# Two-layer FFN, GLA and retention block with an attention block: the sums of seven-product pairs divided anew between VectorE, GpSimd and adding DMAs

## The chip, the core and the metric

The kernel runs on one core of one Trainium2 chip. The metric is the device time of one execution in microseconds (us), as the median of repeated runs. Everything is float32 at the interfaces; nothing is shared with other cores.

## What is computed

The input is one sequence of 256 tokens of width 1024. The first block has two layers; each is FFN, mixer, FFN, with a layer norm after each. The mixer is gated linear attention (GLA) in the first layer and retention in the second. A second block follows: three attention branches, their merge, and a further FFN. The change touches the four FFNs of the first block alone:

```python
def swiglu(x, w_in, w_out):
    gate, up = jnp.split(x @ w_in, 2, axis=-1)
    return (jax.nn.silu(gate) * up) @ w_out

def first_block(x, ffn_w_in, ffn_w_out, ln_g, ln_b,
...
    for i in range(DEPTH):
        h = layer_norm(DN_ALPHA * h + 0.5 * swiglu(h, ffn_w_in[i, 0], ffn_w_out[i, 0]), ln_g[i, 0], ln_b[i, 0])
...
        h = layer_norm(DN_ALPHA * h + 0.5 * swiglu(h, ffn_w_in[i, 1], ffn_w_out[i, 1]), ln_g[i, 2], ln_b[i, 2])
```

The width of an FFN's hidden layer is 2816.

## The kernel before

**Tiles and parts.** All weights come as a stream of tiles of 128 x 2048 float32 (1 MB), read by DMAs of the SyncE queue into raw slots. Each float32 is computed with as two reduced parts: ScalarE writes the hi part of a tile (`split_hi`, line 609), VectorE writes lo = raw - hi (`split_lo`, line 1174), and TensorE adds three products, hi by hi, hi by lo and lo by hi. The activations are split in the same way. A tile can be multiplied by its hi part as soon as ScalarE is done, and by its lo part as soon as VectorE is.

**An FFN** has 11 steps of 256 hidden columns (f = 0 to 3 counts the FFNs). A step computes gate and up, `hidden` (line 1293) multiplies silu(gate) by up on VectorE, TensorE transposes the result (`turn_hidden`, line 2209), ScalarE and VectorE split it again (`hidden_hi`, `hidden_lo`), and a `down` product (lines 1988 to 1992) adds it into the output. Steps 0, 1, 4, 7 and 10 are computed in one of the plain ways. In `features_both` (lines 2097 and 2101) the hi weights are multiplied by x hi and x lo side by side, 512 columns, and the lo weights by x hi, 256 columns; ScalarE then copies the half that belongs to x lo out of PSUM and VectorE adds it to the other half (`summed_step`, line 1350), before the silu. In `features_unit` three products of 256 columns add up in PSUM, with no copy and no sum.

**Pairs.** Steps 2 and 3, 5 and 6, 8 and 9 (`GROUPS`) are computed as pairs, each as a product of two 2 x 2 block matrices with seven block products instead of eight. For this, sums of weight tiles and sums of blocks of x are needed. With b11, b12, b21 and b22 the four weight tiles of a pair, the operands of the products are, in order,

- product 1: b11; product 2: t1 = b11 + b12; product 3: b21; product 4: t2 = t1 + b22; product 5: b22; product 6: t3 = t2 - b11; then a down product; product 7: t4 = t2 + b21 in b21's place; then the second down product.

Each sum is made in the raw slot of one of its operands, and is then split into hi and lo as any other tile. The other operands of products 2, 4, 5 and 6 are the four "forms", combinations of blocks of x, with a hi and a lo part each, which all three pairs of an FFN share. `product` (lines 2236, 2237 and 2240) issues eight matmuls with the hi tile, then waits for lo and issues four.

**Who makes the sums before.** t1: an adding DMA in GpSimd's queue (`add_t1`, lines 500 to 506), issued when both tiles have landed. t2 and t3: VectorE (lines 1344 and 1368). t4: an adding DMA in GpSimd's queue (`add_t4`, lines 508 to 513). The form sums and form lo's: VectorE (lines 1322 to 1327, and 1334); the form hi's: ScalarE (line 689).

**What sets the order.** Each engine works through its own queue in the order in which the program is written, and waits on semaphores. Around the first pair, ScalarE's order in an FFN is: the hi of step 1's second tile, the four blocks of x kept in SBUF (`keep_x`, line 672; not in the first FFN), b11's hi, the silu of step 0, the four form hi's, t1's hi, step 0's hidden hi, step 1's copies and silu, b21's hi. GpSimd's queue also has the layer norms' inverse roots, the residuals (line 485), a part of one lo split (line 475), and the DMAs that load the next norm's rows (line 480).

## Time and profile before

| | |
|---|---|
| median of 3 runs | 1524.89 us (1524.52 to 1525.26) |
| the profiled execution: own time, and span of its instructions | 1523.43 us, 1521.5 us |
| TensorE matmuls (PE) | 1490.0 us, 98% of the span |
| VectorE (DVE) | 1112.7 us, 73% |
| ScalarE (ACT) | 833.1 us, 55% |
| GpSimd (POOL) | 156.4 us, 10% |
| mean granted TensorE clock | 0.994 |
| chain of waits that ended last | PE 83%, DVE 7%, DMA 6% |
| adding DMAs from a raw_more slot, to landing | 20 of 1 MB, median 7.2 us |
| adding DMAs from a raw slot, to landing | 4 of 1 MB, median 12.3 us |

The profile follows one execution. In a line of a timeline stand the start, the duration, the engine, the line of the kernel, the operation, output<-inputs with shapes, and in brackets the idle time of the engine before it and what ended that; xN stands for N such instructions in a row. Only the time in which the engine with the most work stands still, here TensorE, is time that could be saved without taking work off it. The granted clock is a share of 2.4 GHz; at 0.50 TensorE runs at 1.2 GHz.

### The profile page before, as it was taken

The numbers are of one execution on the slowest core, as the hardware profiler recorded it, in microseconds if no ns is written. First come the engines' busy times: TensorE is split into PE (matmuls) and PEld (weight loads), VectorE is DVE, ScalarE is ACT, GpSimd is POOL, SyncE is SP. The second block draws the span as 40 slices with busy tenths as digits, with TensorE's granted clock in tenths as the row PEclk, the third lists the DMA queues.
The fourth block names the chain that finished last, engine by engine and source line by source line (L and its number), as shares of the span: only waits on it lengthen the run. The fifth ranks groups of instructions, "written<-read, shape, count | busy, mean of one in ns | idle before, by whom it ended". The sixth has DMA issues, their size and how long they took to land.

```text
span 1521.5 us, 18598 instructions
## 1 busy us (share of the span) xinstructions
PE 1490.0 (98%) x7654; PEld 1258.1 (83%) x7654; DVE 1112.7 (73%) x1135; ACT 833.1 (55%) x839; POOL 156.4 (10%) x152
## 2 busy tenths in 40 slices
PE   8899999989999999999999989999999999999997
PEld 6688888878888788888888868888898888888886
DVE  5887687787877977787567787867686556785555
ACT  5656467565565665554434556555636566354443
POOL 0400020110002000024021200002002200020000
PEclk9999999999999999999999999999999999999999
DMA  9777454477837777555544677746444434465551
GB/s 356 268 231 229 182 204 169 150 262 277 295 106 296 218 241 256 166 227 188 179 160 169 224 249 226 269 163 237 154 167 142 164 139 166 166 222 194 193 191 58
DMA packets 46595, 310.08 MB, mean 204 GB/s; under 512 B 5568, under 2 KB 6016, under 8 KB 10800
## 3 DMA queue, kind: packets, MB, share of 16 engines
q1 hardware_dynamic: 38592, 270.35, 47.8%
q0 software_dynamic: 6112, 34.80, 9.9%
q10 hardware_dynamic: 1808, 3.74, 0.6%
q8 instruction: 61, 1.00, 0.3%
q14 instruction: 22, 0.18, 0.0%
HBM read 282.60 MB, written 1.05 MB: 186 GB/s over the span
## 4 chain that ended last, share of the span: by engine, by line
PE 83%; DVE 7%; DMA 6%; issue 1%; ACT 1%; POOL 1%; SPq 0%; POOLq 0%; DVEq 0%; ACTq 0%
PE psum L1988 16%; PE psum L1992 15%; PE psum L1991 15%; PE psum L2097 7%; PE psum L2124 6%; PE psum L2101 4%; DVE weights_lo L1174 4%; DMA weights_raw_more<-weights_raw_more 3%; PE psum L2240 3%; PE psum L2237 3%; PE psum L2236 3%; PE psum L2131 3%; DMA weights_raw_more<-in_weights 2%; PE psum L2020 1%; PE psum L2033 1%
## 5 line engine op out<-in xcount | busy, mean ns | idle before, releaser
L1174 DVE TENSOR_TENSOR weights_lo<-weights_raw,weights_hi 128x2048 fp32r<-128x2048 f32 x191 | 440.9, 2312 | 198.0 <-ACT weights_hi L609 196.6
L609 ACT ACTIVATE weights_hi<-weights_raw 128x2048 fp32r<-128x2048 f32 (+1 forms) x198 | 372.4, 1883 | 194.9 <-PE psum L1992 136.2
L1174 DVE TENSOR_TENSOR weights_lo<-weights_raw_more,weights_hi 128x2048 fp32r<-128x2048 f32 x56 | 128.2, 2289 | 70.5 <-ACT weights_hi L609 70.5
L1988 PE MATMUL psum<-weights_hi,hidden_hi 128*128 128x512 f32 x416 | 163.9, 394 | 3.3 <-DVE weights_lo L1174 3.3
L1991 PE MATMUL psum<-weights_lo,hidden_hi 128*128 128x512 f32 x416 | 162.4, 390 | 0.0
L1992 PE MATMUL psum<-weights_hi,hidden_lo 128*128 128x512 f32 x416 | 162.1, 390 | 0.0
L1988 PE MATMUL psum<-weights_hi,operand 128*128 128x512 f32 x384 | 151.5, 394 | 0.0
L1991 PE MATMUL psum<-weights_lo,operand 128*128 128x512 f32 x384 | 149.8, 390 | 0.0
L609 ACT ACTIVATE weights_hi<-weights_raw_more 128x2048 fp32r<-128x2048 f32 x56 | 107.1, 1913 | 70.1 <-DMA weights_raw_more<-weights_raw_more 39.2
L1992 PE MATMUL psum<-weights_hi,operand 128*128 128x512 f32 x352 | 137.2, 390 | 0.0
L2097 PE MATMUL psum<-operand,weights_hi 128*128 128x512 f32 x544 | 129.4, 390 | 0.0
L2097 PEld LDWEIGHTS psum<-operand,weights_hi 128*128 128x128 f32 x544 | 101.2, 188 | 20.4
L2124 PE MATMUL psum<-operand,weights_hi 128*128 128x512 f32 x384 | 96.5, 393 | 0.0
L1988 PEld LDWEIGHTS psum<-weights_hi,hidden_hi 128*128 128x128 f32 x416 | 78.2, 188 | 20.4 <-issue 5.2
L1992 PEld LDWEIGHTS psum<-weights_hi,hidden_lo 128*128 128x128 f32 x416 | 78.1, 188 | 16.3
L1991 PEld LDWEIGHTS psum<-weights_lo,hidden_hi 128*128 128x128 f32 x416 | 78.2, 188 | 15.2
L1988 PEld LDWEIGHTS psum<-weights_hi,operand 128*128 128x128 f32 x384 | 72.1, 188 | 15.8 <-issue 1.3
L1991 PEld LDWEIGHTS psum<-weights_lo,operand 128*128 128x128 f32 x384 | 72.2, 188 | 14.2
L2124 PEld LDWEIGHTS psum<-operand,weights_hi 128*128 128x128 f32 x384 | 69.4, 189 | 13.3 <-issue 0.3
L1992 PEld LDWEIGHTS psum<-weights_hi,operand 128*128 128x128 f32 x352 | 66.1, 188 | 13.9
L1174 DVE TENSOR_TENSOR weights_lo_more<-weights_raw_more,weights_hi_more 128x2048 fp32r<-128x2048 f32 x32 | 73.4, 2292 | 1.7 <-ACT weights_hi_more L609 1.7
L2101 PEld LDWEIGHTS psum<-operand,weights_lo 128*128 128x128 f32 x544 | 69.7, 191 | 2.6
(386 smaller groups left out, 2799.9 us busy)
## 6 DMA issues: line engine op xcount, KB each, us to landing
weights_raw<-in_weights SPq DMA_DIRECT2D x198, 1024.0 KB, 4.8
weights_raw_more<-in_weights SPq DMA_DIRECT2D x56, 1024.0 KB, 8.9
weights_raw_more<-weights_raw_more POOLq DMA_DIRECT2D x20, 1024.0 KB, 7.2
ln_rows<-in_ln_rows POOLq DMA_DIRECT2D x16, 512.0 KB, 7.3
weights_raw_more<-weights_raw POOLq DMA_DIRECT2D x4, 1024.0 KB, 12.3
weights_raw<-in_weights SPq DMA_DIRECT2D x4, 256.0 KB, 4.3
weights_raw<-in_weights SPq DMA_DIRECT2D x2, 512.0 KB, 6.7
normalised<-in_x POOLq DMA_DIRECT2D x2, 512.0 KB, 11.1
```

The costliest lines, as they stand in the source:

```text
L609: nc.scalar.activation(hi[:, rest], whole[:, rest], ACT.Copy).then_inc(hi_split, 1)
L1174: nc.vector.tensor_tensor(lo_of(n), raw_of(n), hi_of(n).bitcast(F32), ALU.subtract).then_inc(lo_split, 1)
L1988: mm(out, a_hi, b_hi, start=start, stop=False, skip_group_check=True)
L1991: mm(out, a_hi, b_lo, start=False, stop=False, skip_group_check=True)
L1992: return mm(out, a_lo, b_hi, start=False, stop=stop, skip_group_check=True)
L2097: mm(banks[b // 2][:, b % 2, :], w_hi_n[:, cols], x_both[:, c, :, :].rearrange("p a t -> p (a t)"), start=c == 0, stop=False, skip_group_c ...
L2101: last = mm(banks[b // 2][:, b % 2, 0:TOK], w_lo_n[:, cols], x_hi[:, c, :], start=False, stop=c == KC - 1, skip_group_check=True)
L2124: mm(banks[half][:, b, :], w_hi_n[:, cols], x_both[:, c, :, :].rearrange("p a t -> p (a t)"), start=c == 0, stop=False, skip_group_check=True)
L2131: last = mm(banks[half][:, b, 0:TOK], w_lo_n[:, cols], x_hi[:, c, :], start=False, stop=c == KC - 1, skip_group_check=True)
L2236: mm(work[:, b, :], a_hi, w_hi_n[:, cols], start=start and k == 0, stop=False, skip_group_check=True)
L2237: mm(work[:, b, :], a_lo, w_hi_n[:, cols], start=False, stop=False, skip_group_check=True)
L2240: last = mm(work[:, b, :], a_hi, w_lo_n[:, cols], start=False, stop=k == 3, skip_group_check=True)
```

## The change

The form sums (now five instructions) and the four form lo's go from VectorE to GpSimd (`first_forms`), in all four FFNs. t1 goes from an adding DMA to VectorE (`add_t1`), t3 from VectorE to GpSimd (`add_t3`); t2 stays on VectorE, t4 an adding DMA. Step 1 goes from `features_both` to `features_unit`. ScalarE makes the form hi's in the order 0, 3, 2, 1. Line numbers of the changed kernel are 2 to 26 higher.

```diff
+FORM_ORDER, FORM_SUMS = (0, 3, 2, 1), (1, 5, 4, 2)
...
                     for tb in range(TB):
                         residual(tb, ALPHA if ln < 6 else ALPHA_2)
-                    if LAYER_STARTS[ln] in FFN_STARTS:
-                        add_t1(LAYER_STARTS[ln], FFN_STARTS.index(LAYER_STARTS[ln]), GROUPS[0])
                     load_rows(ln + 1)
...
+            def first_forms(f):
...
+                x11, x12, x21, x22 = x_part(0, 0), x_part(0, 1), x_part(1, 0), x_part(1, 1)
+                nc.gpsimd.tensor_tensor(x22, x22, x21, ALU.subtract).then_inc(form_summed, 1)
+                nc.gpsimd.tensor_tensor(x21, x11, x21, ALU.subtract).then_inc(form_summed, 1)
+                pool.wait_ge(form_summed, 5 * f + 1)
+                nc.gpsimd.tensor_tensor(x11, x22, x11, ALU.add).then_inc(form_summed, 1)
...
+                for at, k in enumerate(FORM_ORDER):
+                    pool.wait_ge(form_hi_done, 4 * f + at + 1)
+                    nc.gpsimd.tensor_tensor(by_chunk(form_lo(k)), in_form[k], by_chunk(form_hi(k)).bitcast(F32),
+                                            ALU.subtract).then_inc(form_ready, 1)
+
+            def add_t3(n0, f, s):
...
-                for load in (n, n + 1):
-                    pool.wait_ge(weight_loaded[RAW_SLOT[LOAD_OF[load]]], RAW_COUNT[LOAD_OF[load]])
-                pool.dma_start(raw_of(n + 1), raw_of(n), accum_op=ALU.add).then_inc(t1_added, 16)
+                t2, t3 = raw_of(n + 1), raw_of(n + 5)
+                pool.wait_ge(lo_split, n + 1)
+                pool.wait_ge(tile_added, tile_sums(f, s) + 1)
+                nc.gpsimd.tensor_tensor(t3, t2, t3, ALU.subtract).then_inc(t3_added, 1)
...
             def add_tiles(n0, f):
 
+                first_forms(f)
                 for s in GROUPS:
-                    if s != GROUPS[0]:
-                        add_t1(n0, f, s)
+                    add_t3(n0, f, s)
                     add_t4(n0, f, s)
...
                     split_hi(n + 4)
                     copy_back(n + 2, p5[:, :], 1)
-                    split_hi(n + 5, (tile_added, 2 * g + 2))
+                    split_hi(n + 5, (t3_added, g + 1))
...
-                summed_step(1, n0 + 4, 2)
+                act.wait_ge(weights_used, n0 + 4)
+                nc.scalar.activation(silu_g[:, :, :], two(pairs[1][:, 0, :]), ACT.Silu).then_inc(silu_done, 1)
+                split_hi(n0 + 6)
+                act.wait_ge(hid_done, j0 + 2)
+                hidden_hi(j0 + 1, 1, hid[:, 0:2, :])
...
+                def add_t1(s):
+                    b11, b12 = loaded(("up", s, 0)), loaded(("up", s + 1, 0))
+                    nc.vector.tensor_tensor(b12, b12, b11, ALU.add).then_inc(tile_added, 1)
...
                     split_lo(n + 3)
-                    add_t3()
                     split_lo(n + 4)
...
                 split_lo(n0 + 3)
-                form_sums()
                 hidden(j0, pairs[0][:, :, TOK:2 * TOK])
+                add_t1(2)
                 split_lo(n0 + 4)
-                forms_lo()
                 split_lo(n0 + 5)
                 hidden_lo(j0, 0, two(acc[:, 3, :]))
-                summed_step(1, 2)
+                add_t2(2)
+                dve.wait_ge(hid_ready, j0 + 1)
+                hidden(j0 + 1, two(pairs[1][:, 1, :]))
+                split_lo(n0 + 6)
+                hidden_lo(j0 + 1, 1, hid[:, 0:2, :])
...
                         split_lo(ahead - 1)
+                        if after in GROUPS:
+                            add_t1(after)
                         split_lo(ahead)
...
-                features_both(n0 + 2, unit_banks(1), between=lambda: turn_hidden(j0, 2 * P, acc[:, 3:4, :]), second_free=kept)
+                features_unit(n0 + 2, pairs[1], between={4: turn_first})
...
                     if before == 1:
                         first_free = lambda: None
-                        second_free = lambda: pe.wait_ge(gate_summed, summed_before(f, 2))
+                        second_free = lambda: pe.wait_ge(hid_done, j0 + 2)
```

**VectorE's queue, first pair of the first FFN, before.** The names: `weights_lo` and `weights_lo_more` are written by lo splits, L1322 to L1327 are the form sums, L1334 the form lo's, L1344 is t2.

```order
L1322 TENSOR_TENSOR normalised<-normalised 128x4x128 [waits x_lo_done]
L1323 TENSOR_TENSOR normalised<-normalised 128x4x128
L1325 SCALAR_TENSOR_TENSOR normalised<-normalised 128x4x128 [waits dve_step]
L1327 SCALAR_TENSOR_TENSOR normalised<-normalised 128x4x128 [waits dve_step]
L1293 TENSOR_TENSOR hidden<-silu_gate,psum 128x512 [waits silu_done]
L1174 TENSOR_TENSOR weights_lo<-weights_raw_more,weights_hi 128x2048 [waits hi_split]
L1334 TENSOR_TENSOR hidden_lo<-normalised,hidden_hi 128x512 [waits form_hi_done] x3
L1334 TENSOR_TENSOR form4_lo<-normalised,form4_hi 128x512 [waits form_hi_done]
L1174 TENSOR_TENSOR weights_lo<-weights_raw_more,weights_hi 128x2048 [waits hi_split]
L1300 TENSOR_TENSOR hidden_lo<-psum,hidden_hi 128x512 [waits hid_hi_done]
L1350 TENSOR_TENSOR gate_up<-psum,gate_up 128x512 [waits against_lo_copied] x2
L1344 TENSOR_TENSOR weights_raw_more<-weights_raw_more,weights_raw 128x2048 [waits weight_loaded0]
```

Behind these follow hidden of step 1, b21's lo, its hidden lo, t2's lo, and t3 (L1368).

**VectorE's queue at the same place, now.** L1348 is t1, L1352 is t2, L1200 a lo split (b11 and t1, then b21, then t2, then b22).

```order
L1319 TENSOR_TENSOR hidden<-silu_gate,psum 128x512 [waits silu_done]
L1348 TENSOR_TENSOR weights_raw_more<-weights_raw_more 128x2048 [waits weight_loaded5,weight_loaded4]
L1200 TENSOR_TENSOR weights_lo<-weights_raw_more,weights_hi 128x2048 [waits hi_split] x2
L1326 TENSOR_TENSOR hidden_lo<-psum,hidden_hi 128x512 [waits hid_hi_done]
L1352 TENSOR_TENSOR weights_raw_more<-weights_raw_more,weights_raw 128x2048 [waits weight_loaded0]
L1319 TENSOR_TENSOR hidden<-silu_gate,psum 128x512 [waits silu_done,hid_ready]
L1200 TENSOR_TENSOR weights_lo<-weights_raw_more,weights_hi 128x2048 [waits hi_split]
L1326 TENSOR_TENSOR hidden_lo<-hidden,hidden_hi 128x512 [waits hid_hi_done]
L1200 TENSOR_TENSOR weights_lo_more<-weights_raw_more,weights_hi_more 128x2048 [waits hi_split]
L1200 TENSOR_TENSOR weights_lo<-weights_raw,weights_hi 128x2048 [waits hi_split]
```

Form sums, form lo's, the two sums of step 1 and t3 are gone from it, and t1 has come in behind the first hidden.

**GpSimd's queue, from the norm ahead of the second FFN (f = 1), now.** L508 to L515 are the form sums, L518 the form lo's, L527 is t3, L534 t4's adding DMA.

```order
L487 TENSOR_SCALAR residual<-normalised 128x1024
L482 DMA ln_rows<-in_ln_rows 128x1024 x2
L508 TENSOR_TENSOR normalised<-normalised 128x4x128 [waits x_kept]
L509 TENSOR_TENSOR normalised<-normalised 128x4x128
L511 TENSOR_TENSOR normalised<-normalised 128x4x128 [waits form_summed]
L513 TENSOR_TENSOR normalised<-normalised 128x4x128 [waits form_summed]
L515 TENSOR_SCALAR normalised<-normalised 128x4x128 [waits form_summed]
L518 TENSOR_TENSOR hidden_lo<-normalised,hidden_hi 128x512 [waits form_hi_done]
L518 TENSOR_TENSOR form4_lo<-normalised,form4_hi 128x512 [waits form_hi_done]
L518 TENSOR_TENSOR hidden_lo<-normalised,hidden_hi 128x512 [waits form_hi_done] x2
L527 TENSOR_TENSOR weights_raw_more<-weights_raw_more 128x2048 [waits tile_added,lo_split]
L534 DMA weights_raw_more<-weights_raw_more 128x2048 [waits tile_added,lo_split]
```

Before, t1's adding DMA stood between the residuals and the norm's rows, and behind the rows came t4's; now nine operations on the forms and t3 stand there.

## Rows read from the trace of the kernel before

**Rows 1.** Waits of PE by line and releaser: total us, times, longest us.

```profile
PE psum L2236 <- ACT weights_hi L609: 9.8, 5, 2.6
```

**Rows 2.** Table by windows: busy us and instructions by engine, PE clock, DMA share.

```profile
24.40:60.00 35.60, 27.59 (x112) 20.83 (x113) 27.14 (x20) 18.56 (x18) 14.15 (x6) 0.90 0.75 243
...
310.70:360.00 49.30, 44.90 (x208) 35.87 (x207) 40.09 (x35) 28.90 (x31) 2.43 (x4) 0.97 0.83 279
...
491.00:540.00 49.00, 46.40 (x224) 38.18 (x223) 42.67 (x36) 31.67 (x34) 6.14 (x6) 1.00 0.76 247
...
871.00:920.00 49.00, 44.13 (x204) 35.58 (x203) 38.96 (x34) 27.50 (x29) 2.46 (x4) 0.97 0.81 277
```

**Rows 3.** Timeline of PE in FFN0, around its first wait.

```profile
24.37 0.66 PE L2209 MATMUL psum<-constants,hidden 128*128 128x128 f32 x4 [1.85 <-DVE hidden L1293]
24.78 5.50 PE L2097 MATMUL psum<-operand,weights_hi_more 128*128 128x512 f32 x16
```

**Rows 4.** Timeline of PE in FFN1: step 1, then products 1 to 3.

```profile
310.70 3.79 PE L2097 MATMUL psum<-operand,weights_hi 128*128 128x512 f32 x16
...
316.24 0.60 PE L2209 MATMUL psum<-constants,hidden 128*128 128x128 f32 x4
...
322.25 0.40 PE L2236 MATMUL psum<-weights_hi,operand 128*128 128x512 f32 x1
...
325.09 0.47 PE L2236 MATMUL psum<-weights_hi,hidden_hi 128*128 128x512 f32 x1
...
331.08 0.48 PE L2236 MATMUL psum<-weights_hi,operand 128*128 128x512 f32 x1 [2.54 <-ACT weights_hi L609]
```

**Rows 5.** Timeline of GpSimd between norm and FFN1, two windows.

```profile
305.01 1.06 POOL L485 TENSOR_SCALAR residual<-normalised 128x1024 f32<-128x1024 f32 x1 [3.44 <-DVE normalised L1235]
...
305.01 4.12 POOL L485 TENSOR_SCALAR residual<-normalised 128x1024 f32<-128x1024 f32 x2 [3.44 <-DVE normalised L1235]
309.38 0.94 POOL L506 DMA_DIRECT2D weights_raw_more<-weights_raw_more  x1 [0.26 <-issue]
```

**Rows 6.** Timeline of ScalarE in FFN1: x kept, t1's hi, b21's hi.

```profile
309.15 2.07 ACT L672 ACTIVATE normalised<-psum 128x512 f32<-128x512 f32 x4 [0.40 <-POOL residual L485]
...
323.03 1.92 ACT L609 ACTIVATE weights_hi<-weights_raw_more 128x2048 fp32r<-128x2048 f32 x1 [6.84 <-DMA weights_raw_more<-weights_raw_more]
...
329.04 1.89 ACT L609 ACTIVATE weights_hi<-weights_raw_more 128x2048 fp32r<-128x2048 f32 x1
```

**Rows 7.** Timeline of VectorE in FFN1: a lo split, and t2.

```profile
305.43 2.77 DVE L1174 TENSOR_TENSOR weights_lo<-weights_raw,weights_hi 128x2048 fp32r<-128x2048 f32 x1
...
328.99 2.28 DVE L1344 TENSOR_TENSOR weights_raw_more<-weights_raw_more,weights_raw 128x2048 f32<-128x2048 f32 x1
```

**Rows 8.** Timeline of PE: first of 48 narrow matmuls, and the next after.

```profile
174.48 0.28 PE L1988 MATMUL psum<-operand,weights_hi 128*128 128x256 f32 x1
...
180.24 0.40 PE L1988 MATMUL psum<-weights_hi,hidden_hi 128*128 128x512 f32 x1
```

**Rows 9.** Timeline of VectorE, FFN1's second pair: t1's lo, t2's lo.

```profile
371.44 2.29 DVE L1174 TENSOR_TENSOR weights_lo<-weights_raw_more,weights_hi 128x2048 fp32r<-128x2048 f32 x1 [3.68 <-ACT weights_hi L609]
...
380.45 2.28 DVE L1174 TENSOR_TENSOR weights_lo_more<-weights_raw_more,weights_hi_more 128x2048 fp32r<-128x2048 f32 x1
```

**Rows 10.** Timeline of GpSimd in retention: pairs of 512-column products.

```profile
774.57 2.55 POOL L559 TENSOR_TENSOR ret_g<-ret_g,ret_rot 128x512 f32<-128x512 f32 x2 [45.80 <-ACTq L925]
...
801.71 3.53 POOL L559 TENSOR_TENSOR ret_g<-ret_g,ret_rot 128x512 f32<-128x512 f32 x2 [7.05 <-ACTq L925]
```

**Rows 11.** Groups of GpSimd by form: busy us, mean ns, idle before.

```profile
L475 POOL TENSOR_TENSOR weights_lo<-weights_raw,weights_hi 128x1024 fp32r<-128x1024 f32 x7 | 16.8, 2403 | 35.8 <-ACT weights_hi L607 34.2 <-DVE normalised L1235 1.6
```

**Rows 12.** Timeline of VectorE beside the products at 801.71.

```profile
804.01 3.38 DVE L1174 TENSOR_TENSOR weights_lo<-weights_raw,weights_hi 128x2048 fp32r<-128x2048 f32 x1
```

**Rows 13.** Timeline of PE, FFN1's second pair: lo part of t2's product.

```profile
386.98 1.07 PE L2240 MATMUL psum<-weights_lo_more,hidden_hi 128*128 128x512 f32 x4
```

**Rows 14.** Timeline of GpSimd in FFN0: residuals behind t4's adding DMA.

```profile
47.81 12.04 POOL L485 TENSOR_SCALAR residual<-normalised 128x1024 f32<-128x1024 f32 x2
```

More of the change, by code:

```diff
@@ L375, in build @@
         group_index = lambda f, s: len(GROUPS) * f + GROUPS.index(s)
+        tile_sums = lambda f, s: 2 * (len(GROUPS) * f + GROUPS.index(s)) + 1
         against_hi, against_lo = (lambda t: t[:, :, 0:TOK]), (lambda t: t[:, :, TOK:2 * TOK])
-        summed_before = lambda f, j: SUMMED * f + sum(1 for s in range(1, j) if s not in GROUPS and s - 1 not in GROUPS)
+        summed_before = lambda f, j: SUMMED * f + sum(1 for s in range(2, j) if s not in GROUPS and s - 1 not in GROUPS)
         gate_of = lambda j: pairs[1] if j == 1 else pairs[0]
@@ L532, in _ @@
             for s in GROUPS[1:]:
-                add_t1(N_FFN0, 0, s)
+                add_t3(N_FFN0, 0, s)
                 add_t4(N_FFN0, 0, s)
@@ L685, in forms_hi @@
                 def forms_hi():
-                    for k in range(4):
-                        act.wait_ge(form_summed, 4 * f + k + 1)
+                    for k in FORM_ORDER:
+                        act.wait_ge(form_summed, 5 * f + FORM_SUMS[k])
                         nc.scalar.activation(by_chunk(form_hi(k)), in_form[k], ACT.Copy).then_inc(form_hi_done, 1)
@@ L1313, in last_step @@
                     hidden_lo(j0 + j, j % 3, hid[:, 0:2, :])
-                def form_sums():
-                    if f:
-                        dve.wait_ge(x_kept, 4 * f)
-                    else:
-                        dve.wait_ge(x_lo_done, KC // 2)
-                    x11, x12, x21, x22 = x_part(0, 0), x_part(0, 1), x_part(1, 0), x_part(1, 1)
-                    first = mark(nc.vector.tensor_tensor(x22, x22, x21, ALU.subtract))
-                    second = mark(nc.vector.tensor_tensor(x21, x11, x21, ALU.subtract))
-                    dve.wait_ge(dve_step, first)
-                    third = mark(nc.vector.scalar_tensor_tensor(out=x11, in0=x22, scalar=-1.0, in1=x11, op0=ALU.mult, op1=ALU.subtract))
-                    dve.wait_ge(dve_step, third)
-                    nc.vector.scalar_tensor_tensor(out=x12, in0=x12, scalar=-1.0, in1=x11, op0=ALU.mult,
-                                                   op1=ALU.subtract).then_inc(form_summed, 4)
-                def forms_lo():
-                    for k in range(4):
-                        dve.wait_ge(form_hi_done, 4 * f + k + 1)
-                        nc.vector.tensor_tensor(by_chunk(form_lo(k)), in_form[k], by_chunk(form_hi(k)).bitcast(F32),
-                                                ALU.subtract).then_inc(form_ready, 1)
                 def loaded(load):
@@ L2218, in ffn, with turn_first @@
                 unit_banks = lambda j: (gate_of(j), up_of(j))
[L2219 to L2220 removed]
+                def turn_first():
+                    if f:
+                        pe.wait_ge(x_kept, 4 * f)
+                    turn_hidden(j0, 2 * P, acc[:, 3:4, :])
+                features_unit(n0 + 2, pairs[1], between={4: turn_first})
                 def next_down(j, n, hooks={}):
                     pe.wait_ge(hid_ready, j0 + j + 1)
[L2225 to L2226 removed]
+                    if j == 0 and f:
+                        pe.wait_ge(x_kept, 4 * f)
                     at = 2 * (j % 3)
```

30 lines of the change are left out of this document (16 added, 14 removed).

## The prediction, on record before the result

> **What bounds the kernel now.** The page's busy shares come first: TensorE works 98% of the span, so the time moves only by TensorE's own work, by its waits, or by its clock. The table of waits then names what it waits for; its largest line is the first matmul of a block product, line 2236, which waits for a hi part by ScalarE, 9.8 us in five waits [rows 1]. The table by windows puts the waits in one place of each FFN, its first pair of steps: the four windows there hold 35.60-27.59 = 8.0, 49.30-44.90 = 4.4, 49.00-46.40 = 2.6 and 49.00-44.13 = 4.9 us without TensorE [rows 2], together **19.9 us**. Two prices hang on a long wait: the idle time, and the clock after it. The granted clock is 1.00 in the third window, but 0.90 in the first and 0.97 in the others [rows 2]; right behind the wait of 1.85 us at 24.37, sixteen wide matmuls took 5.50 us, where sixteen take 3.79 in FFN1 [rows 3, 4]. So such a stretch at half speed costs about **1.7 us**. The windows' clocks fit four of them, two in FFN0 and one each in FFN1 and FFN3.
>
> **What FFN1 waits for today.** The adding DMA of t1 is issued at 309.38 [rows 5], and ScalarE gets to split t1 at 323.03 [rows 6], 13.6 us later. VectorE then does t1's lo, a hidden lo, the two sums of step 1, t2 and the next hidden. ScalarE can't split b21 before 329.04 [rows 6], since the silu of step 1 stands ahead of it and waits for those sums. That is the 2.54 us before 331.08 [rows 4]; the other 1.9 of the 4.4 are lo's that VectorE, running without a pause, delivers late.
>
> **The change, part by part.** The parts meet in one chain, so I cost each and then walk the chain for FFN1.
>
> *Step 1 in plain products.* Today's first tile of step 1, 16 wide and 16 narrow matmuls, ran from 310.70 to 316.24 = 5.54 us [rows 4], so 11.08 for two. In come 96 matmuls of 256 columns; 48 of them took 180.24-174.48 = 5.76 [rows 8], so 11.52. **+0.44 us per FFN**, straight on TensorE, 1.8 in all. In return two copies leave ScalarE, two sums leave VectorE, and the silu waits for TensorE alone.
>
> *t1 on VectorE, its DMA gone.* 2.28 us, as t2 [rows 7], against 13.6 from issue to use. In pairs 5 and 8 it stands in a queue that has 3.68 us of pause ahead of 371.44 [rows 9]: free there. In pair 2 it stands behind the first hidden.
>
> *Form sums and form lo's on GpSimd.* Two 512-column products took 2.55 us there, 1.28 each [rows 10]; the fifth sum has one input, about 0.6 as an estimate from 1.06 for 1024 columns [rows 5]. So 4x1.28+0.6 = 5.7 us of sums and 5.1 of lo's. VectorE gets rid of eight ops per FFN, and hidden is no longer behind four of them.
>
> *t3 on GpSimd.* The trace has no such op of 2048 columns with two inputs. 1024 columns took 2.40 [rows 11], 512 took 1.28, so each further 512 adds 1.12, which makes **about 4.6 us**, an estimate; its floor is VectorE's 2.28. The Trainium skill, "GPSIMD Engine Reference", section "3.1 Elementwise — side-by-side cycle accounting", speaks against such a move: it has 4497 ns for this size against VectorE's 2293; by it t3 would be 0.1 us shorter and the sum below 0.4 less.
>
> *Do the two engines run side by side?* The rows say no, where VectorE's op has two inputs in SBUF. The split at 305.43 took 2.77 us, with a GpSimd residual under way at its start, and GpSimd's two residuals 4.12 instead of twice 1.06 [rows 5, 7]. Around 802 the pair of products took 3.53 instead of 2.55, and the split at 804.01 took 3.38 [rows 10, 12]: whoever comes second waits until the other's op is over, and GpSimd can get in between two VectorE ops. The Trainium skill, "SBUF — State Buffer", section "SBUF: two separate sides", has this as a rule (one port pair, held for a whole instruction); these rows agree, and without the lock the time would be that of the first rival. Ops with an operand in PSUM (hidden, the first hidden lo) I take as free of it.
>
> *The chain for FFN1, letting the two alternate.* The keeping of x ends at 309.15+2.07 = 311.2 [rows 6]. Sums 1 to 3 run on GpSimd to 315.1. VectorE's t1, ready at 314.1 behind hidden, runs 315.1 to 317.3; sum 4 to 318.6; b11's lo to 320.8; sum 5 to 321.4. ScalarE makes the four form hi's in order, the last by 322.0, and only then t1's hi, done by 323.9; today it is 323.03+1.92 = 324.9 [rows 6]. Of the DMA's 13.6 us **one** comes through. VectorE: t1's lo to 326.2; t2, behind the third form lo, 327.5 to 329.8; hidden to 330.4. TensorE leaves step 1 at 322.25+0.44 = 322.7, takes 325.09-322.25 = 2.84 per product [rows 4], and is ready for product 3 at 328.4. That product waits until hidden has read its bank, 330.5: **2.1 us**. The last form lo holds VectorE until 331.1, so b21's lo is there at 333.3, **1.0 late**. Then t3 has the port, 333.3 to 337.9, and behind it stand VectorE's hidden lo and t2's lo, done at 340.7. TensorE has issued t2's first eight matmuls by 336.0: **4.7 us**. After that VectorE keeps ahead, since t3 is off its queue. Together 7.8 us. The bounds for each of the three waits: 0, if GpSimd's ops fall into VectorE's pauses, and some 7 us more in all if it is kept waiting (third rival).
>
> In pairs 5 and 8 the same t3 meets slack: t2's lo was ready at 380.45+2.28 = 382.7 and used at 386.98, 4.2 us early [rows 9, 13]; against 4.6 that leaves 0.4 at most, and I book nothing. The adding DMA of t4 now stands behind t3 on GpSimd, some 4 us later than today; ScalarE splits t4 as the second last tile of the group, so I book nothing. Without that cover it would be those 4 us.
>
> **The sum.** Each FFN: 0.44 and the new waits, less the old, with the clock. FFN1: 0.44+7.8-4.4 = +3.8, half speed once in both. FFN2: 0.44+7.8-2.6, and 1.7 for a stretch at half speed that it lacks today: +7.3. FFN3: 0.44+7.8-4.9 = +3.3. FFN0: hidden waits for the silu alone (0.5 off the 1.85), t1's wait goes, t3 holds up b21's lo by some 3.1; 0.44+1.4+3.1-8.0 = -3.1, half speed twice in both. In all **+11.3 us**. The profiled execution's own time is 1523.4, 1.5 under the median of 1524.9; on the median that is 1536.2, and with the 0.4 of a pair left open, **1537 us**. Less than 0.2%, 3 us, can't be told from no change here.
>
> **Rivals.**
> *Faster: GpSimd keeps clear of VectorE.* Place: pair 2 of each FFN; what decides is whether t3 is over when VectorE comes to t2's lo. Then all waits go but FFN0's 1.4 for hidden, with three of the four stretches at half speed: 1524.9-19.9-5.1+1.8+1.4 = 1503 us. For it: each part takes work off the queue that TensorE waits for. Against it: rows 5, 7, 10 and 12, as above. Chance 0.24.
> *No change.* The alternation falls better: product 3 and b21's lo aren't waited for, t3's 4.7 stay in each FFN. 4x(4.7+0.44) = 20.6 for 19.9: 1526 us. Chance 0.09.
> *Slower still: GpSimd starts late.* FFN0's two residuals, directly behind an adding DMA in GpSimd's queue, took 12.04 us [rows 14] against 4.12 in FFN1: 8 us more, in which VectorE ran op upon op. In FFN1 to 3 the form sums now stand directly behind the two DMAs of the norm's rows. Late by 8, t1's hi comes 7 us after today's, three times: +21, 1558 us. Chance 0.15.
>
> **How the numbers follow.** My own case has 0.52 and spans 1528 to 1548, a wait of 2 us more or less in each FFN. The range reaches to both sides, 1506 to 1560; it leaves out half of the faster rival and a third of the slowest, under 0.2. Faster by over 0.2%: 0.24; within it: 0.09; slower: 0.52+0.15 = 0.67.
>
> **What would show it.** Right: TensorE's waits sit at the first pairs again, the longest for VectorE's lo of t2, with a GpSimd op of 4.6 us ahead of it; lo splits of over 4 us on VectorE; t1's hi hardly earlier than today. Wrong: splits that stay at 2.29 while GpSimd runs (faster), or form sums that begin microseconds after x is kept (third rival). Waits in pairs 5 and 8, or for t4's DMA, would show a cost that I booked at nothing.

## The result, and the profile after

The changed kernel takes 1529.72 us (median of 6 runs, 1527.92 to 1531.03) against 1524.99 us for the kernel before in the same runs (1523.22 to 1526.00). The ratio is 1.0033 with a 95% interval of 1.0022 to 1.0043: slower, by 4.7 us or 0.33%. The forecast was slower by 12 us. The profiled execution's own time is 1527.92 us, its span 1525.9 us.

The page's first part, for TensorE, VectorE and GpSimd:

```profile
PE 1494.7 (98%) x7782; PEld 1271.1 (83%) x7782; DVE 1158.2 (76%) x1095; ACT 829.7 (54%) x831; POOL 269.8 (18%) x188
```

(One line of the page holds all engines.) TensorE works 1494.7 us where it worked 1490.0, and stands idle 1525.9-1494.7 = 31.2 us where it stood idle 31.5. So TensorE waits as long as before, and works 4.7 us longer: 4 x 0.4 for the plain step 1, the rest with a lower clock, 0.988 in the mean for 0.994. Behind that stand larger gains and losses, as the stages show. The residuals of each layer norm mark the ends of the stages in GpSimd's timeline. Before:

```profile
203.02 4.10 POOL L485 TENSOR_SCALAR residual<-normalised 128x1024 f32<-128x1024 f32 x2 [2.78 <-DVE normalised L1235]
...
489.34 4.10 POOL L485 TENSOR_SCALAR residual<-normalised 128x1024 f32<-128x1024 f32 x2 [2.78 <-DVE normalised L1235]
...
670.56 4.10 POOL L485 TENSOR_SCALAR residual<-normalised 128x1024 f32<-128x1024 f32 x2 [2.79 <-DVE normalised L1235]
...
864.79 4.13 POOL L485 TENSOR_SCALAR residual<-normalised 128x1024 f32<-128x1024 f32 x2 [2.78 <-DVE normalised L1235]
...
1050.43 4.11 POOL L485 TENSOR_SCALAR residual<-normalised 128x1024 f32<-128x1024 f32 x2 [2.79 <-DVE normalised L1235]
```

and after:

```profile
197.84 4.09 POOL L487 TENSOR_SCALAR residual<-normalised 128x1024 f32<-128x1024 f32 x2 [2.78 <-DVE normalised L1261]
...
300.09 4.12 POOL L487 TENSOR_SCALAR residual<-normalised 128x1024 f32<-128x1024 f32 x2 [3.45 <-DVE normalised L1261]
...
486.47 4.10 POOL L487 TENSOR_SCALAR residual<-normalised 128x1024 f32<-128x1024 f32 x2 [2.78 <-DVE normalised L1261]
...
673.91 4.10 POOL L487 TENSOR_SCALAR residual<-normalised 128x1024 f32<-128x1024 f32 x2 [2.78 <-DVE normalised L1261]
...
868.15 4.11 POOL L487 TENSOR_SCALAR residual<-normalised 128x1024 f32<-128x1024 f32 x2 [2.78 <-DVE normalised L1261]
...
1055.82 4.10 POOL L487 TENSOR_SCALAR residual<-normalised 128x1024 f32<-128x1024 f32 x2 [2.78 <-DVE normalised L1261]
```

With the row at 305.01 before [rows 5], the differences of these starts, after less before, are -5.18, -4.92, -2.87, +3.35, +3.36 and +5.39 us. Across the two mixers between the FFNs the difference hardly moves (+0.26 and +0.01); across the FFNs it does:

| | forecast | measured, by these rows | TensorE's waits before | after |
|---|---|---|---|---|
| FFN0 | -3.1 | -5.2 | 8.0 + 1.85 | 2.38 + 3.57 + 0.53 |
| FFN1 | +3.8 | +2.0 | 4.4 | 2.65 + 2.67 |
| FFN2 | +7.3 | +6.2 | 2.6 | 2.28 + 3.20 |
| FFN3 | +3.3 | +2.0 | 4.9 | 2.28 + 3.69 |
| sum | +11.3 | +5.1 | 21.7 | 23.3 |

Some 0.9 us come off again behind the last FFN, in work that the change doesn't touch; that was not followed. The table of TensorE's waits after, which answers to [rows 1] (line, releaser, total us, times, longest us):

```profile
PE psum L2252 <- DVE weights_lo L1200: 13.1, 4, 3.7
PE psum L2248 <- DVE hidden L1319: 7.2, 3, 2.7
PE psum L1996 <- DVE weights_lo L1200: 2.9, 2, 2.4
```

The waits for ScalarE's hi are gone. In their place stand three for `hidden` at product 3, and one per FFN for b21's lo. (The 2.4 us of the last line are in FFN0, for the lo of step 1's first tile, which a plain step needs at its first matmuls already.) How they come about in FFN1, first on GpSimd:

```profile
306.39 1.30 POOL L508 TENSOR_TENSOR normalised<-normalised 128x512 f32<-128x512 f32 x1 [1.07 <-ACT normalised L694]
...
310.29 3.22 POOL L513 TENSOR_TENSOR normalised<-normalised 128x512 f32<-128x512 f32 x1
313.60 2.54 POOL L515 TENSOR_SCALAR normalised<-normalised 128x512 f32<-128x512 f32 x1
...
318.64 4.58 POOL L518 TENSOR_TENSOR hidden_lo<-normalised,hidden_hi 128x512 fp32r<-128x512 f32 x2
325.51 4.57 POOL L527 TENSOR_TENSOR weights_raw_more<-weights_raw_more 128x2048 f32<-128x2048 f32 x1 [2.29 <-DVE weights_raw_more L1352]
```

then on ScalarE (t1's hi) and VectorE (t1's lo, t2, hidden, b21's lo, t2's lo):

```profile
316.71 1.90 ACT L631 ACTIVATE weights_hi<-weights_raw_more 128x2048 fp32r<-128x2048 f32 x1
```

```profile
318.65 3.42 DVE L1200 TENSOR_TENSOR weights_lo<-weights_raw_more,weights_hi 128x2048 fp32r<-128x2048 f32 x1 [2.98 <-ACT weights_hi L631]
...
322.59 2.78 DVE L1352 TENSOR_TENSOR weights_raw_more<-weights_raw_more,weights_raw 128x2048 f32<-128x2048 f32 x1
325.29 0.68 DVE L1319 TENSOR_TENSOR hidden<-silu_gate,psum 128x512 f32<-128x512 f32 x1
325.89 6.34 DVE L1200 TENSOR_TENSOR weights_lo<-weights_raw_more,weights_hi 128x2048 fp32r<-128x2048 f32 x1
...
332.75 2.28 DVE L1200 TENSOR_TENSOR weights_lo_more<-weights_raw_more,weights_hi_more 128x2048 fp32r<-128x2048 f32 x1
```

and on TensorE (product 3, its first matmul and its lo part):

```profile
326.02 0.79 PE L2248 MATMUL psum<-weights_hi,operand 128*128 128x512 f32 x1 [2.65 <-DVE hidden L1319]
...
332.28 1.76 PE L2252 MATMUL psum<-weights_lo,operand 128*128 128x512 f32 x4 [2.67 <-DVE weights_lo L1200]
```

The fourth sum took 3.22 us instead of 1.29 and the fifth 2.54 instead of the 0.6 that was estimated, since VectorE's t1 and b11's lo held the port. So ScalarE is done with t1's hi only at 318.6. VectorE's t1 lo took 3.42 beside a form lo. `hidden` ends at 326.0, and product 3 starts then, 2.65 us late. GpSimd's t3 starts at 325.51, as soon as t2 is there, runs 4.57 us, and b21's lo takes 6.34 instead of 2.29: it stands still until t3 is over. The matmuls of product 3 wait 2.67 us for it. Behind both waits TensorE runs at half speed:

```profile
326.00:329.40 3.40, 3.38 (x8) 2.48 (x8) 3.40 (x1) 3.40 (x4) 3.40 (x1) 0.52 0.00 0
332.20:336.20 4.00, 3.92 (x10) 3.14 (x11) 4.00 (x4) 0.80 (x1) 0.93 (x1) 0.57 0.64 131
```

(columns as in [rows 2]; the granted clock is 0.52 and 0.57 of 2.4 GHz, so mostly the lower of its two levels, 1.2 GHz). Each of the last three FFNs has two such stretches now; the first of them is shorter in FFN2 and FFN3.

### The profile page after: what moved, and what is told of

Its sections match the earlier page's. It is cut to its first block, busy times and chain, and to the rows that moved or that the text cites. A ratio compares the mean times of both kernels' runs of the same rounds, so it can differ in the third digit from the quotient of the medians.

```text
span 1525.9 us, 18855 instructions
## 1 busy us (share of the span) xinstructions
PE 1494.7 (98%) x7782; PEld 1271.1 (83%) x7782; DVE 1158.2 (76%) x1095; ACT 829.7 (54%) x831; POOL 269.8 (18%) x188
## 4 chain that ended last, share of the span: by engine, by line
PE 90%; DVE 4%; POOL 2%; ACT 1%; issue 1%; DMA 1%; SPq 0%; POOLq 0%; DVEq 0%; ACTq 0%
PE psum L1996 16%; PE psum L2000 16%; PE psum L1999 16%; PE psum L2105 7%; PE psum L2132 6%; PE psum L2252 5%; PE psum L2248 4%; PE psum L2249 4%; PE psum L2109 4%; PE psum L2139 3%; DVE weights_lo L1200 2%; PE psum L2028 1%; PE psum L2041 1%; PE psum L2034 1%; DMA weights_raw_more<-in_weights 1%
## 5 line engine op out<-in xcount | busy, mean ns | idle before, releaser
L1200 DVE TENSOR_TENSOR weights_lo<-weights_raw,weights_hi 128x2048 fp32r<-128x2048 f32 x191 | 441.4, 2315 | 201.1 <-ACT weights_hi L631 199.6
L1200 DVE TENSOR_TENSOR weights_lo<-weights_raw_more,weights_hi 128x2048 fp32r<-128x2048 f32 x56 | 189.1, 3384 | 21.3 <-ACT weights_hi L631 21.3
L2105 PE MATMUL psum<-operand,weights_hi 128*128 128x512 f32 x480 | 114.2, 390 | 0.0
L2105 PEld LDWEIGHTS psum<-operand,weights_hi 128*128 128x128 f32 x480 | 89.2, 188 | 17.9
L469 POOL TENSOR_TENSOR ln_rstd<-ln_rstd,minus_half 128x1 f32<-128x1 f32 x16 | 8.9, 557 | 536.4 <-ACT ln_rstd L658 536.4
L2132 PE MATMUL psum<-operand,weights_hi 128*128 128x512 f32 x384 | 96.5, 393 | 0.0
L2000 PEld LDWEIGHTS psum<-weights_hi,hidden_lo 128*128 128x128 f32 x416 | 78.1, 188 | 16.3
L1999 PEld LDWEIGHTS psum<-weights_lo,hidden_hi 128*128 128x128 f32 x416 | 78.2, 188 | 15.3
L2132 PEld LDWEIGHTS psum<-operand,weights_hi 128*128 128x128 f32 x384 | 69.4, 189 | 13.3 <-issue 0.3
L1996 PE MATMUL psum<-operand,weights_hi 128*128 128x256 f32 x256 | 73.7, 288 | 2.4 <-DVE weights_lo L1200 2.4
```

The source lines that it names most:

```text
L1200: nc.vector.tensor_tensor(lo_of(n), raw_of(n), hi_of(n).bitcast(F32), ALU.subtract).then_inc(lo_split, 1)
L1996: mm(out, a_hi, b_hi, start=start, stop=False, skip_group_check=True)
L1999: mm(out, a_hi, b_lo, start=False, stop=False, skip_group_check=True)
L2000: return mm(out, a_lo, b_hi, start=False, stop=stop, skip_group_check=True)
L2105: mm(banks[b // 2][:, b % 2, :], w_hi_n[:, cols], x_both[:, c, :, :].rearrange("p a t -> p (a t)"), start=c == 0, stop=False, skip_group_c ...
L2132: mm(banks[half][:, b, :], w_hi_n[:, cols], x_both[:, c, :, :].rearrange("p a t -> p (a t)"), start=c == 0, stop=False, skip_group_check=True)
```

## The experiments

All are timed in five rounds against the kernel before, whose medians there were 1524.1 to 1524.5 us; the row of the changed kernel is the result above. The ones that leave out parts of the change, and which parts each has:

| | t1 | step 1 | forms | t3 | us | ratio to before, 95% interval |
|---|---|---|---|---|---|---|
| before | DMA | sums | VectorE | VectorE | 1524 | 1 |
| changed kernel | VectorE | plain | GpSimd | GpSimd | 1529.7 | 1.0033 (1.0022 to 1.0043) |
| t3 back | VectorE | plain | GpSimd | VectorE | 1516.3 | 0.9948 (0.9935 to 0.9962) |
| forms back | VectorE | plain | VectorE | GpSimd | 1515.1 | 0.9940 (0.9927 to 0.9952) |
| both back | VectorE | plain | VectorE | VectorE | **1501.1** | 0.9850 (0.9836 to 0.9863) |
| t1 alone | VectorE | sums | VectorE | VectorE | 1506.8 | 0.9883 (0.9868 to 0.9898) |
| step 1 alone | DMA | plain | VectorE | VectorE | 1522.7 | 0.9987 (0.9978 to 0.9996) |
| sums on GpSimd | VectorE | plain | sums GpSimd | VectorE | 1508.0 | 0.9891 (0.9878 to 0.9905) |
| lo's on GpSimd | VectorE | plain | lo's GpSimd | VectorE | 1507.3 | 0.9888 (0.9875 to 0.9902) |
| t3 on GpSimd in later pairs | VectorE | plain | VectorE | first pair VectorE | 1501.4 | 0.9849 (0.9836 to 0.9862) |

### t3 back on VectorE

```diff
-                    add_t3(n0, f, s)
...
                     split_lo(n + 3)
+                    add_t3()
```

> The changed kernel with t3 back on VectorE, behind t2's lo as before; forms stay on GpSimd, t1 on VectorE, step 1 plain. Theory A (GpSimd's ops hold the shared port against VectorE's splits): the four waits for b21's lo (13.1 us in all, 2.7 to 3.7 each) go, with the half-speed stretch behind each (about 1.6), and the small waits for later lo's come back (about 1 us per FFN); the waits for hidden at product 3 (7.2 us) stay, since GpSimd's form ops still delay t1. 13 + 6 - 4 = 15 us less: about 1515 us. Theory B (the loss is TensorE's own work, plain step 1 and clock, and the waits only move from one engine to another): 1528 to 1532 us, the b21 waits replaced by waits of the same size for t2's lo or t3.

1516.3 us: theory A. The waits for b21's lo are gone, the three for `hidden` stay. Of the 4.8 us in the second line, 3.0 are a new wait in FFN0, for b22's lo:

```profile
PE psum L2242 <- DVE hidden L1308: 7.2, 3, 2.7
PE psum L2246 <- DVE weights_lo L1189: 4.8, 4, 3.0
PE psum L1990 <- DVE weights_lo L1189: 4.2, 4, 2.5
```

### The forms back on VectorE

```diff
-                first_forms(f)
...
                 split_lo(n0 + 3)
+                form_sums()
                 hidden(j0, pairs[0][:, :, TOK:2 * TOK])
                 add_t1(2)
                 split_lo(n0 + 4)
+                forms_lo()
```

> The changed kernel with the form sums and form lo's back on VectorE in their old order; t3 stays on GpSimd. Theory A (the port): t1's hi no longer stands behind five GpSimd sums, so it is done some 5 us earlier, t2 and hidden follow, and the three waits for hidden at product 3 go; t3 then gets the port some 4 us earlier as well and is over by the time TensorE needs b21's lo, so most of the 13.1 us go too: 1503 to 1510 us. Theory C (t3's length of 4.6 us costs by itself, wherever it starts): the waits for b21's lo stay at about 3 us each, only 7 us go: 1520 to 1524 us. Theory B: 1527 to 1531 us.

1515.1 us lies between the forecasts, a miss for all three. The waits are those of theory C: the ones for `hidden` go, those for b21's lo stay, as 13.3 us in four.

```profile
PE psum L2253 <- DVE weights_lo L1177: 13.3, 4, 4.2
```

```profile
318.80 2.28 DVE L1351 TENSOR_TENSOR weights_raw_more<-weights_raw_more,weights_raw 128x2048 f32<-128x2048 f32 x1
320.99 0.68 DVE L1296 TENSOR_TENSOR hidden<-silu_gate,psum 128x512 f32<-128x512 f32 x1
321.59 6.40 DVE L1177 TENSOR_TENSOR weights_lo<-weights_raw_more,weights_hi 128x2048 fp32r<-128x2048 f32 x1
```

With the forms away t2 is earlier, but TensorE's product 3 and GpSimd's t3 are both earlier with it: t3 starts when t2 ends, `hidden`, which reads PSUM, runs its usual 0.68 us beside it, and b21's lo meets t3 as before (6.40 us). So here this wait does not depend on what the forms do. The span fell by 13.4 us all the same: 7.6 are idle time (1512.5-1488.9 = 23.6 for 31.2), and 5.8 TensorE's work (1488.9 for 1494.7 us), at a clock of 0.993 for 0.988.

### Both back on VectorE: t1 and step 1 alone are left

Both edits above together.

> The changed kernel with the forms and t3 back on VectorE: what is left of the change is t1 on VectorE instead of an adding DMA, and the plain step 1. Theory A: nothing on GpSimd holds the port in a pair, t1 is there early, so the waits for product 3 and b21 go; small waits for lo's behind t3 may remain, under 1 us per FFN: 1503 to 1510 us. Theory B (the 4.7 us are TensorE's own work in step 1 and the clock): no faster than the kernel before, 1525 to 1530 us.

1501.1 us, 23 us and 1.5% faster than before: theory A, and the fastest kernel of this study. TensorE's work falls to 1483.2 us at a clock of 0.999, and of the waits only small ones are left:

```profile
PE psum L1991 <- DVE weights_lo L1166: 3.7, 5, 1.5
PE psum L2247 <- DVE weights_lo L1166: 3.6, 4, 1.4
```

So the two parts that the change puts on GpSimd cost 15.2 us (forms) and 14.0 us (t3), each measured against this kernel. Together they cost some 28 us, since the changed kernel is 4.7 us slower than the one before and this one 23.0 faster; and the two other parts bring 23.

### t1 alone, and step 1 alone

Both edits are made in the kernel before. For the first, `add_t1` on GpSimd becomes an addition on VectorE:

```diff
-                pool.dma_start(raw_of(n + 1), raw_of(n), accum_op=ALU.add).then_inc(t1_added, 16)
...
+                    nc.vector.tensor_tensor(b12, b12, b11, ALU.add).then_inc(t1_added, 16)
...
                 hidden(j0, pairs[0][:, :, TOK:2 * TOK])
+                add_t1(2)
                 split_lo(n0 + 4)
```

> The kernel before with one part of the change alone: t1 on VectorE behind the first hidden, and behind the first of two lo splits ahead of the later pairs; step 1 stays with its copies and sums, forms and t3 stay on VectorE. Theory D (the landing of t1's adding DMA set the waits of the first pairs): t1's hi is done some 10 us earlier, b21's hi in time, nearly all waits of the first pairs go but FFN0's 1.85 for hidden: 1500 to 1506 us. Theory E (step 1's copies, sums and silu ahead of b21's hi set them): most waits stay, 1518 to 1524 us.

1506.8 us, 0.8 above theory D's range, so a narrow miss, and far from theory E: t1 alone brings 17.6 us. For the second, only step 1 changes:

```diff
-                summed_step(1, 2)
+                add_t2(2)
+                dve.wait_ge(hid_ready, j0 + 1)
+                hidden(j0 + 1, two(pairs[1][:, 1, :]))
...
-                features_both(n0 + 2, unit_banks(1), between=lambda: turn_hidden(j0, 2 * P, acc[:, 3:4, :]), second_free=kept)
+                features_unit(n0 + 2, pairs[1], between={4: turn_first})
```

> The kernel before with the plain step 1 alone: t1 stays an adding DMA, forms and t3 stay on VectorE. Theory D: t1's hi comes no earlier, t1's lo and t2 neither, and the hidden of step 1 stands behind t2, so product 3 still waits 2 to 3 us per FFN, now for hidden; plus 0.44 per FFN of TensorE's work: 1520 to 1527 us. Theory E: 1505 to 1512 us.

1522.7 us, theory D: TensorE waits for `hidden` and for t1's hi instead of for b21's hi.

```profile
PE psum L2249 <- DVE hidden L1298: 6.0, 4, 2.2
PE psum L2249 <- ACT weights_hi L610: 6.0, 3, 3.7
```

Behind an early t1, though, the plain step is worth more: 1506.8 to 1501.1.

### Is it the port, or the slow engine's late result?

To the kernel with both back, a GpSimd addition of t3's size is added in t3's place. It doubles b11 in its slot, and VectorE's t3 takes half of it off again, so VectorE keeps all its work and nobody needs the doubling early.

```diff
+                nc.gpsimd.tensor_tensor(b11, b11, b11, ALU.add).then_inc(kept_b11, 1)
...
-                        nc.vector.tensor_tensor(t3, t2, t3, ALU.subtract).then_inc(t3_added, 1)
+                        dve.wait_ge(kept_b11, g + 1)
+                        nc.vector.scalar_tensor_tensor(out=t3, in0=t3, scalar=-0.5, in1=t2, op0=ALU.mult, op1=ALU.add).then_inc(t3_added, 1)
```

> The kernel with forms and t3 on VectorE (1501 us), to which a GpSimd op of t3's size is added in t3's place, that nobody needs early: b11 is doubled in its slot by an addition, and VectorE's t3 takes half of it off again. VectorE keeps all of its own work. Theory A (the port): b21's lo is held up by some 4 us as in the changed kernel, waits of about 3 us per FFN come back with a half-speed stretch behind each: 1513 to 1519 us. Theory F (t3 costs because its result comes late from a slow engine, not by the port): nobody waits for the doubling, 1501 to 1503 us.

1520.2 us: 19 us for an operation that nobody waits for early, 1 us above theory A's range and nothing like theory F. The lo's of block products are waited for again:

```profile
PE psum L2259 <- DVE weights_lo L1177: 10.8, 5, 3.2
```

VectorE, which keeps t3 here, is late for plain products too, with thirteen waits of 6.4 us together where the kernel without the doubling has five of 3.7; that fits the excess over A, but was not taken apart. The two rows of FFN1:

```profile
322.86 3.60 POOL L506 TENSOR_TENSOR weights_raw_more<-weights_raw_more 128x2048 f32<-128x2048 f32 x1 [16.27 <-DVE weights_raw_more L1351]
```

```profile
323.23 5.38 DVE L1177 TENSOR_TENSOR weights_lo<-weights_raw_more,weights_hi 128x2048 fp32r<-128x2048 f32 x1
```

b21's lo takes 5.38 us and ends when GpSimd's 3.60 us and then its own 2.28 are over. So what costs is what the prediction calls the port: GpSimd's op holds up VectorE's split, whoever needs its result. The late result is not needed for it.

### The order that the prediction assumed

In the changed kernel t3 got the port ahead of b21's lo; the prediction had it behind. Here it is put behind:

```diff
-                pool.wait_ge(lo_split, n + 1)
+                pool.wait_ge(lo_split, n + 3)
```

> The changed kernel, with t3 on GpSimd made to wait until b21's lo is done, which is the order that the prediction assumed. If the prediction's chain is right but for that order: the waits for b21's lo fall to under 1 us each and waits of 4 to 5 us for t2's lo come in their place; the end of t2's product moves by 1 us or less per FFN, so the time stays within 4 us of the changed kernel, 1526 to 1531 us. If the order itself was what made the forecast too long: 6 us or more above the changed kernel, 1536 us.

1527.2 us (ratio 1.0022, 1.0013 to 1.0031): the first branch, and no slower than the changed kernel (1.0033; the intervals overlap). The waits are the predicted ones in kind: none for b21's lo, one per FFN for t2's lo. In size they are not, 3.10 us in FFN1 where 4.7 was forecast, and 2.92 to 3.97 in all four:

```profile
326.57 0.79 PE L2248 MATMUL psum<-weights_hi,operand 128*128 128x512 f32 x1 [2.65 <-DVE hidden L1319]
...
335.98 1.57 PE L2252 MATMUL psum<-weights_lo_more,hidden_hi 128*128 128x512 f32 x4 [3.10 <-DVE weights_lo_more L1200]
```

```profile
326.44 2.28 DVE L1200 TENSOR_TENSOR weights_lo<-weights_raw_more,weights_hi 128x2048 fp32r<-128x2048 f32 x1
...
329.24 6.69 DVE L1200 TENSOR_TENSOR weights_lo_more<-weights_raw_more,weights_hi_more 128x2048 fp32r<-128x2048 f32 x1
```

So the order isn't why the forecast was too long.

### Sums or lo's: which part of the forms?

The five sums alone on GpSimd, an edit of the kernel with t3 back:

```diff
-                    nc.gpsimd.tensor_tensor(by_chunk(form_lo(k)), in_form[k], by_chunk(form_hi(k)).bitcast(F32),
...
+                        nc.vector.tensor_tensor(by_chunk(form_lo(k)), in_form[k], by_chunk(form_hi(k)).bitcast(F32),
...
                 split_lo(n0 + 4)
+                forms_lo()
```

and the four lo's alone, an edit of the kernel with both back (`first_forms` then holds the lo's only):

```diff
+                first_forms(f)
...
                 split_lo(n0 + 4)
-                forms_lo()
```

> The kernel with forms and t3 on VectorE (1501 us), with the five form sums alone on GpSimd; the four form lo's stay on VectorE. Theory A1 (of the 15 us that the forms on GpSimd cost, most come through the sums: ScalarE makes t1's hi only behind the last form hi, so t1's lo, t2 and the hidden of step 1 all shift): t1's hi is as late as with all forms on GpSimd, VectorE's ops behind it are 1 us less held up, product 3 waits 1 to 2 us instead of 2.3 to 2.7 per FFN: 1509 to 1514 us. Theory A2 (the lo's do it, by holding the port against t1's lo and t2): 1500 to 1504 us.

> The kernel with forms and t3 on VectorE (1501 us), with the four form lo's alone on GpSimd; the sums stay on VectorE. Theory A1: the form hi's and t1's hi are early, GpSimd's lo's run while TensorE still has step 1 ahead of it, nobody waits for them: 1499 to 1504 us. Theory A2: 1511 to 1516 us.

1508.0 and 1507.3 us: neither theory. Each half costs 6 to 7 us, and both together 15. With the sums there, product 3 waits for `hidden` again, but 1.03 us in FFN1 instead of 2.65. With the lo's there, three of them stretch over 9.82 us, taking turns with VectorE's ops, and TensorE's waits for lo's rise to 10.4 us from 7.3:

```profile
308.57 9.82 POOL L504 TENSOR_TENSOR hidden_lo<-normalised,hidden_hi 128x512 fp32r<-128x512 f32 x3 [4.47 <-ACT hidden_hi L686]
318.36 3.35 POOL L504 TENSOR_TENSOR form_lo<-normalised,form_hi 128x512 fp32r<-128x512 f32 x1
```

### t1's hi ahead of the form hi's

In the kernel with t3 back (1516.3), ScalarE's order is swapped:

```diff
+                second_of_next(2, n0 + 5)
                 forms_hi()
-                second_of_next(2, n0 + 5)
```

> The kernel with all forms on GpSimd and t3 on VectorE (1516 us), with one swap in ScalarE's order: t1's hi ahead of the form hi's. Theory A1: t1's hi is done some 5 us earlier, behind t1's own addition alone; t1's lo, t2 and the hidden of step 1 follow, the waits at product 3 go (7 us, and what hangs on them by the clock): 1502 to 1508 us. If the port alone holds up t1's lo and t2, or the form hi's, now later, are missed by products 2 or 4: 1514 to 1520 us.

1512.4 us: between the two, a miss. The waits at product 3 are gone, so t1's hi was late through ScalarE's order, as theory A1 says. But the last form lo's now come late for product 4. The table names ScalarE's copy for it, which was over at 326.3; GpSimd's last lo ended at 321.60+5.01 = 326.61, and product 4 starts 0.1 us behind that.

```profile
321.60 5.01 POOL L518 TENSOR_TENSOR hidden_lo<-normalised,hidden_hi 128x512 fp32r<-128x512 f32 x2
```

```profile
326.71 0.47 PE L2242 MATMUL psum<-weights_hi_more,hidden_hi 128*128 128x512 f32 x1 [1.69 <-ACT product L726]
```

### t3 on GpSimd in the later pairs only

```diff
                     split_lo(n + 3)
+                    if s == GROUPS[0]:
+                        nc.vector.tensor_tensor(t3, t2, t3, ALU.subtract).then_inc(t3_added, 1)
```

with `add_t3` on GpSimd for the other two pairs.

> The kernel with forms and t3 on VectorE (1501 us), with t3 on GpSimd in the second and third pair of each FFN only. The prediction booked those at nothing, since t2's lo is 4.2 us early there: 1499 to 1503 us, no waits in those pairs. If the port costs there too, 1.2 to 3 us for each of the eight: 1510 us or more.

1501.4 us, the same as 1501.1: the slack that was booked as 4.2 us covers a GpSimd op of 4.9 there, and taking t3 off VectorE there is worth nothing either.

### t3 one lo split later

In the kernel with both back, VectorE makes b22's lo before t3:

```diff
                     split_lo(n + 3)
-                    add_t3()
                     split_lo(n + 4)
+                    add_t3()
```

> The kernel with forms and t3 on VectorE (1501 us), with t3 one lo split later: behind b22's lo instead of ahead of it. The waits of 0.6 to 1.4 us for b22's lo and of 0.55 for the down product's lo should go, if t3's hi then still comes in time: 1496 to 1499 us. If t3's hi is late by VectorE's 2.3 us and ScalarE's 1.9, product 6 waits 1 to 3 us per FFN instead: 1501 to 1508 us.

1513.5 us (ratio 0.9926, 0.9913 to 0.9938): the second branch, and worse than its range. Product 6 waits 2.14 to 2.91 us per FFN; the table names a copy by ScalarE, which stands behind t3's hi in its queue. So the small waits for later lo's are the cheaper price here.

## Why the prediction was wrong

**What held.** The direction, and the chain. Step 1 took 317.71-305.77 = 11.94 us in FFN1 for 11.55 before: +0.39, booked 0.44. t3 took 4.57 to 4.60 in the first pairs, booked 4.6. FFN1 starts 4.93 us earlier now, at 305.77 for 310.70; put into these times, the chain had t1's hi done at 319.0 (measured 318.6), t2 done at 324.9 (325.4), product 3 at 325.6 (326.0), a wait of 2.1 (2.65, and 2.28 twice). Pairs 5 and 8 cost nothing. The port does what the rows said: the doubling of b11 shows it apart from everything else. The Trainium skill, "SBUF — State Buffer", section "SBUF: two separate sides", states that lock for a whole instruction. The traces agree: a split of 2.29 us took 6.34 and 6.40 beside a GpSimd op of 4.57 and 4.61.

**What failed is the sum, in its term "less the old".** It takes off the old waits of TensorE by their idle time, 8.0, 4.4, 2.6 and 4.9 us, with one stretch at half speed where there was one. They had cost more.

In FFN0 the window that gave 8.0 starts at 24.4, while the 1.85 us for `hidden` lie ahead of it [rows 2, 3]; their successor of 1.4 was then charged as new. With the 1.85, FFN0 comes to -5.0 instead of -3.1. It measured -5.2, though not by those waits alone: the one for `hidden` is gone, and 2.38 us for a lo of step 1, which nobody had booked, have come.

For the other three, take the time from the first matmul of product 1 to the first of the down product, which is six products. Without a wait they take 393.32-377.00 = 16.3 us (FFN1's second pair, kernel before). What goes beyond that was lost to waits and clock:

| | before | lost | booked | after | lost | booked |
|---|---|---|---|---|---|---|
| FFN1 | 345.83-322.25 = 23.58 | 7.3 | 4.4+1.7 = 6.1 | 343.07-317.71 = 25.36 | 9.0 | 7.8+1.7 = 9.5 |
| FFN2 | 527.05-507.28 = 19.77 | 3.4 | 2.6 | 530.47-504.82 = 25.65 | 9.3 | 7.8+1.7 = 9.5 |
| FFN3 | 906.87-882.74 = 24.13 | 7.8 | 4.9+1.7 = 6.6 | 912.42-886.52 = 25.90 | 9.6 | 7.8+1.7 = 9.5 |

The new side was booked right to half a microsecond in each FFN, 28.5 us for 27.9 in all. The old side was booked too small by 0.8 to 1.2 us in each, 15.3 for 18.5. With FFN0's 1.85 these make 5.6 of the 6.2 us between the forecast +11.3 and the measured +5.1. FFN2 shows the reason by itself, since its granted clock before is 1.00 [rows 2]. Before:

```profile
507.28 0.40 PE L2236 MATMUL psum<-weights_hi,operand 128*128 128x512 f32 x1
...
514.34 0.39 PE L2237 MATMUL psum<-weights_hi,operand 128*128 128x512 f32 x1
515.34 1.20 PE L2240 MATMUL psum<-weights_lo,operand 128*128 128x512 f32 x4 [0.62 <-DVE weights_lo L1174]
...
527.05 0.47 PE L1988 MATMUL psum<-weights_hi,hidden_hi 128*128 128x512 f32 x1 [0.57 <-DVE weights_lo L1174]
```

and after:

```profile
504.82 0.40 PE L2248 MATMUL psum<-weights_hi,operand 128*128 128x512 f32 x1
...
530.47 0.39 PE L1996 MATMUL psum<-weights_hi,hidden_hi 128*128 128x512 f32 x1
```

Three waits with 2.6 us of idle time cost 3.4 us there. The last matmul ahead of the first of them starts at 514.34 and lasts 0.39 us, and without a wait the next one starts 0.23 us behind it (377.00 and 377.23 in the second pair of FFN1); so 0.16 us of the wait count as busy. The four matmuls behind it take 1.20 us, where four take 1.07 without a wait [rows 13]. Together that is some 0.3 us per wait that no idle time shows. The kernel before has five, three and four waits in these places, the changed kernel two in each.

The idle time of the new waits did come out smaller, 5.3 to 6.0 us where 7.8 was booked, but hardly any time was saved by that. Product 3 stands behind a wait of over 2 us and runs at half speed, wholly in FFN1 and in part in FFN2 and FFN3, a stretch that the sum does not have. FFN1 with t3 in the predicted order shows the parts. From product 3's start to t2's lo the chain has 340.7-330.5 = 10.2 us, of which TensorE works 4.5 and waits 5.7; measured are 335.98-326.57 = 9.4 us, of which it waits 3.1 and works 6.3. So VectorE came 0.8 us sooner, and TensorE worked 1.8 us longer, at half speed, without ending later for it.

Comparing the ends of the same chain would have come nearer. It has t2's lo at 340.7-310.70 = 30.0 us from the start of FFN1, and with t3 in that order it came at 335.98-306.32 = 29.7. In the kernel before, the same matmuls start at 337.76-310.70 = 27.1. From there to the down product both kernels take 8.1 us. So the chain as walked means +2.9 us for FFN1, and the sum made +3.8 of it; in that order +2.65 was measured to the down product. The waits were added up where the ends should have been compared.

**The order of t3 and b21's lo** was predicted the wrong way round, since the last form lo was over earlier than the chain had it. By the run with t3 behind b21's lo it changes little: 1527.2 us for 1529.7.

**The rivals.** The faster one fell with the splits of 6.3 us, as its own test said. "No change" needed a product 3 that isn't waited for; it waited 2.28 to 2.65 us in three FFNs. The third fell too: the form sums start 1.07 us behind the kept x (306.39), and FFN0's residuals, again directly behind a DMA, take 5.46 us in all. So the 12.04 us before [rows 14] were not the DMA's doing alone.

**What the change as a whole hides:** t1 off the adding DMA is worth 17.6 us alone, and 23 with the plain step 1; the forms and t3 on GpSimd give back 15 and 14. The prediction said that of t1's 13.6 us one comes through. It did not ask what the kernel would be without the two GpSimd parts, and that is a kernel of 1501 us.
